# Retention state updates in sets of four, placed between the projection tiles and inside them

## What is computed

```
def retention_chunk(state, q, k, v):
    inner = einsum('bihd,bjhd->bhij', q, k) * dmask
    o = einsum('bhij,bjhv->bihv', inner, v) + einsum('bihd,bhdv->bihv', q, state) * cross_decay
    new_state = chunk_decay * state + einsum('bjhd,bjhv->bhdv', k * k_decay, v)

def retention_output(o, g, gain, w_out):
    on = normalised(o) * gain
    return (silu(g) * on) @ w_out
```

## Time and profile before

| | us |
|---|---|
| median of three timed runs | 1144.43 |
| lowest and highest | 1143.76, 1145.79 |
| the profiled execution | 1144.84 |
| its span, first to last instruction | 1143.1 |
| PE busy in the span | 1088.0 (95%) |
| DVE, ACT busy | 570.1 (50%), 329.8 (29%) |

### The profile page before, as it was taken

One profiled execution on the slowest core, in us unless ns is written; L12 is line 12 of the kernel. 1 busy time (PEld: TensorE's weight loads), 2 busy tenths in 40 slices (PEclk: granted clock), 3 DMA queues, 4 the chain that ended last, 5 costly groups with the idle time before them and its releaser, 6 DMA issues.

```text
span 1143.1 us, 14367 instructions
## 1 busy us (share of the span) xinstructions
PE 1088.0 (95%) x5508; PEld 640.2 (56%) x5508; DVE 570.1 (50%) x1083; ACT 329.8 (29%) x535; POOL 42.5 (4%) x77
## 2 busy tenths in 40 slices
PE   7999999999999999988999999999999999999991
PEld 6877656646443434335888855456787443434330
DVE  6777585656132323229685337648738223323225
ACT  5335256404111111122444313326414111111110
POOL 1300000000000000000000001111000000000000
PEclk9999999998999999999999999999997999999996
DMA  9525281948499999991433478997558599999961
GB/s 325 167 83 182 95 329 61 380 180 317 197 429 406 429 428 428 429 403 63 147 127 107 141 266 304 361 333 274 185 204 338 212 429 406 431 428 428 429 260 47
DMA packets 62890, 319.72 MB, mean 280 GB/s; under 512 B 5026, under 2 KB 5058, under 8 KB 50418
## 3 DMA queue, kind: packets, MB, share of 16 engines
q1 hardware_dynamic: 54386, 288.93, 63.7%
q0 software_dynamic: 8160, 28.80, 6.8%
q10 hardware_dynamic: 288, 1.23, 0.3%
HBM read 296.05 MB, written 22.89 MB: 279 GB/s over the span
## 4 chain that ended last, share of the span: by engine, by line
PE 87%; DVE 6%; DMA 4%; ACT 1%; issue 1%; POOL 0%; SPq 0%; DVEq 0%; ACTq 0%; POOLq 0%
PE bank L1174 31%; PE bank L1006 18%; PE bank L1035 9%; PE bank L966 4%; DMA ring<-in_w_exp_up 3%; PE bank L1494 3%; PE bank L978 2%; PE bank L1241 2%; PE bank L979 2%; PE bank L1484 1%; PE bank L1511 1%; PE bank L944 1%; PE bank L1310 1%; PE bank L1409 1%; PE bank L1395 1%
## 5 line engine op out<-in xcount | busy, mean ns | idle before, releaser
L1174 PE MATMUL bank<-ring_parts,XTt_parts 128*128 128x512 f32 x576 | 181.9, 397 | 2.2 <-DVE ring_parts L2223 1.0
L1174 PE MATMUL bank<-ring_parts 128*128 128x512 f32 x576 | 181.7, 393 | 0.0
L1006 PE MATMUL bank<-ring,XTt 128*64 128x512 f32 x768 | 168.6, 593 | 1.4 <-DMA ring<-in_w_exp_up 1.4
L1174 PEld LDWEIGHTS bank<-ring_parts,XTt_parts 128*128 128x128 f32 x576 | 106.7, 189 | 31.9 <-issue 9.8
L1174 PEld LDWEIGHTS bank<-ring_parts 128*128 128x128 f32 x576 | 107.9, 189 | 24.4 <-issue 1.8
L1006 PEld LDWEIGHTS bank<-ring,XTt 128*64 128x64 f32 x768 | 55.4, 137 | 108.1 <-issue 106.3
L1035 PE MATMUL bank<-ring,arena 128*64 128x512 f32 x512 | 113.4, 595 | 1.7 <-DMA ring<-in_w_exp_down 1.7
L2041 DVE TENSOR_TENSOR arena<-XTt,bank 128x512 f32<-128x512 f32 x16 | 17.3, 1080 | 193.5 <-PE bank L1006 193.5
L707 DVE TENSOR_TENSOR ring_parts<-ring,ring_parts 128x4096 fp32r<-128x4096 f32 x21 | 92.7, 4419 | 23.1 <-ACT ring_parts L696 23.1
L696 ACT ACTIVATE ring_parts<-ring 128x4096 fp32r<-128x4096 f32 (+1 forms) x29 | 84.5, 2916 | 13.8 <-DMA ring<-in_w_in_ret 6.5
L1663 ACT ACTIVATE arena<-bank 128x512 f32<-128x512 f32 (+6 forms) x116 | 53.5, 489 | 88.9 <-PE bank L1174 49.6
(11 more groups left out here) (261 smaller groups left out, 1287.6 us busy)
## 6 DMA issues: line engine op xcount, KB each, us to landing
ring<-in_w_exp_down SPq DMA_DIRECT2D x32, 2048.0 KB, 14.2
ring<-in_w_exp_up SPq DMA_DIRECT2D x32, 2048.0 KB, 14.9
ring<-in_w_exp_gate SPq DMA_DIRECT2D x16, 2048.0 KB, 14.4
arena<-in_w_exp_gate SPq DMA_DIRECT2D x16, 2048.0 KB, 20.0
ring<-in_w_in_ret SPq DMA_DIRECT2D x12, 2048.0 KB, 10.0
ring<-in_state_ret SPq DMA_DIRECT2D x16, 1024.0 KB, 6.6
out_state_s<-ring POOLq DMA_DIRECT2D x16, 1024.0 KB, 5.9
ring<-in_w_in_attn SPq DMA_DIRECT2D x5, 2048.0 KB, 8.3
```

The lines of the kernel that those rows point to most:

```text
L1006: last = pe.matmul(ps[64 * j:64 * j + 64, :], xs[:, k, x0:x0 + 64], w[:, k, :], start=(k == 0), stop=(k == KC - 1))
L1174: last = pe.matmul(ps[:, 0:width], x(t, a, k), w[c][:, k, 0:width], **at)
```

## The change

The states are no longer worked off eight updates at a time. A list `RETENTION` gives one order for PE, DVE and POOL, in which a state's updates are two sets of four (`("update", s, half)`). The sample products (`("so", s)`) stand by themselves in it. A tile with two more numbers, such as `("tile", 0, 1, 0, 1)`, takes a set (here state 0, half 1) in its middle, after 12 of its 24 products, through the argument `lines` of `project`. `banks_of_set` gives the banks: 3, 4, 5, 2, and for the sets (3, 1), (4, 0) and (7, 0) it gives 5, 0, 1, 2. POOL's stores follow set by set. `keys_of(s + 1)` comes after a state's second set. The first tile of n = 3 now stands in the list, with the last set in it. No product, reading or transfer is added or taken away, and SP's order is as it was.

```
-STATES = [(0, 1), (2, 3, 4), (5, 6, 7)]
+RETENTION = ([("head", 0)]
+             + [("tile", 0, 0), ("so", 0), ("update", 0, 0), ("tile", 0, 1, 0, 1), ("so", 1), ("update", 1, 0), ("tile", 0, 2),
+                ("update", 1, 1), ("head", 1)]
+             + [("tile", 1, 0), ("so", 2), ("update", 2, 0), ("tile", 1, 1, 2, 1), ("tile", 1, 2), ("so", 3), ("update", 3, 0),
+                ("head", 2), ("update", 3, 1), ("so", 4), ("update", 4, 0)]
+             + [("tile", 2, 0, 4, 1), ("so", 5), ("update", 5, 0), ("tile", 2, 1, 5, 1), ("so", 6), ("update", 6, 0), ("tile", 2, 2),
+                ("update", 6, 1), ("head", 3), ("so", 7), ("update", 7, 0), ("tile", 3, 0, 7, 1)])
+def banks_of_set(s, half):
+    return (5, 0, 1, 2) if (s, half) in ((3, 1), (4, 0), (7, 0)) else (3, 4, 5, 2)
...
-            def store_state(s):
-                for half in range(2):
-                    wait_emptied(pool, "update", s, 4 * half + 3)
-                    pool.dma_start(state_rows(O["state_s"], s, half),
-                                   weights(("state", s))[:, 4 * half:4 * half + 4, :]).then_inc(state_stored[s][half], 16)
+            def store_state(s, half):
+                wait_emptied(pool, "update", s, 4 * half + 3)
+                pool.dma_start(state_rows(O["state_s"], s, half),
+                               weights(("state", s))[:, 4 * half:4 * half + 4, :]).then_inc(state_stored[s][half], 16)
...
+            def updates(s, half):
                 if s == 0:
                     pe.wait_ge(twice_ready, 3)
                 pe.wait_ge(kd_ready, s + 2)
-                for j in range(8):
+                for j in range(4 * half, 4 * half + 4):
...
-            def gate(n, t):
+            def gate(n, t, *between):
                 if t == 0:
                     pe.wait_ge(low_ready, NIN - 1 + 8 + n)
-                project(fill(("rin", 8 + n, t)), t, x_parts, parts(("rin", 8 + n))).then_inc(full(("rin", 8 + n, t)), 1)
+                project(fill(("rin", 8 + n, t)), t, x_parts, parts(("rin", 8 + n)),
+                        lines=lambda i: updates(*between) if between and i == 2 else None).then_inc(full(("rin", 8 + n, t)), 1)
...
-            head(0)
-            for n in range(3):
-                gate(n, 0)
-                state(STATES[n][0])
-                gate(n, 1)
-                gate(n, 2)
-                state(STATES[n][1])
-                head(n + 1)
-                for s in STATES[n][2:]:
-                    state(s)
+            for what, *of in RETENTION:
+                if what == "head":
+                    head(*of)
+                elif what == "so":
+                    sample_products(*of)
+                elif what == "update":
+                    updates(*of)
+                else:
+                    gate(*of)
...
+                elif what == "tile":
+                    n, t = of[:2]
+                    if of[2:]:
+                        updated(*of[2:])
+                    if n < 3 and t < 2:
+                        gate(n, t)
+                    elif n < 3:
+                        half(n)
```

## The result

| | before | after |
|---|---|---|
| median of the timed runs, us | 1144.91 (6 runs, 1143.76 to 1147.86) | 1154.00 (6 runs, 1151.16 to 1155.60) |
| ratio to before, 95% interval | | 1.0074 (1.0063 to 1.0086) |
| the profiled execution and its span | 1144.84, 1143.1 | 1154.39, 1152.7 |

The change costs 9.1 us by the medians.

The account below looks back on a forecast made before the run. PE, busy 214.05 of 215.00 us, was taken to bound the stage. Sets save 7.9, cuts cost 1.0 and waits 7.9, giving +1.0; the output projection adds 1.6: +2.6, a median of 1147.0, range 1143.5 to 1150.5.

Parts of the forecast that it names:

- A set of four at 1.91: Retention stage: four updates take PE 1.91 us if nothing holds them; over 16 sets this saves 7.9 us.
- The fourth rival: Every set: DVE's pace binds even with empty banks, 2.36 us a set, 1152.4 us; chance 0.05.
- (a): Tiles (0, 2) and (2, 2), right after sets (1, 0) and (6, 0), wait for bank 2: 3.8 us.
- (b): Sets (1, 1) and (6, 1), right after tiles (0, 2) and (2, 2), wait for bank 2: 1.0 us.
- (c): Tile (1, 0) waits for the rest of its weights, done 10.1 after tile (0, 2): 0.4 us.
- (d): Set (4, 0) waits for its keys, which stand late in DVE's list: 0.7 us.
- (e): Tiles (2, 0) and (3, 0) wait for bank 0, second bank of the sets before them: 1.5 us in all.
- (f): State 5 waits for its slot's store and reload after state 3's late half: 0 to 4.6, taken as 0.5 us.
- The other states have over 5 us to spare: Loads of states other than 5 and 6: over 5 us to spare, with POOL and SP transfers in unchanged sequence.
- The output projection's lag: Output projection: DVE and ACT come 3.6 us later against PE, leaving 1.6 us at the last restart; bounds 0 to 3.6.
- The third: Slower than forecast: states 5 and 6 land by the trace's longer times, +2 to +4, 1149.0 to 1151.0 us; chance 0.13.
- The faster rival: Bank waits (a), (b) and (e), 6.3 us, stay away as DVE's readings stay hidden: 1140.7 us; chance 0.12.

Follow-up runs that it names:

- the edit of set (7, 1) alone: Changed kernel with set (7, 1) ahead of tile (3, 0) and not in its middle: 1150.85 us, ratio 1.0052.
- the last run: Changed kernel with states 2 and 4 in one run, set (3, 1) before head 2, (7, 1) before its tile, other banks: 1140.93 us, ratio 0.9969.
- banks_apart: Changed kernel with other banks for the sets of states 1 and 6, apart from bank 2: 1149.54 us, ratio 1.0051.
- reload_after_both_stores: Changed kernel with neither half of states 2 to 7 loaded before both halves of its slot's forerunner are stored: 1155.25 us, ratio 1.0093.

## Why the prediction was wrong in size and right in sign

**A set of four at 1.91:** right, 1.92 in the chain. The fourth rival, DVE's pace for each set, did not come.

**(a), (b), bank 2:** right. Tiles (0, 2) and (2, 2) stand 1.71 us for line 2504 each (forecast 1.7), set (6, 1) took 2.53 (forecast 2.4), and taking both away gave 4.8 us, as summed.

**(c), the rest of tile (1, 0)'s weights:** forecast ready 10.1 after tile (0, 2) and ready at 10.10 (701.50 less 691.40); PE stood 0.1 for it and not 0.4, since set (1, 1) held it a little longer.

**(d), (e):** right. The timeline of PE in after has the keys ahead of set (4, 0), by 0.57, and bank 0 ahead of tile (2, 0), by 0.60 (in brackets, the idle time before):

```profile
739.15 1.99 PE L1506 MATMUL bank<-arena 64*128 64x512 f32 x8 [0.57 <-DVE arena L2497]
...
741.75 0.70 PE L1184 MATMUL bank<-ring_parts,XTt_parts 128*128 128x512 f32 x2 [0.60 <-DVE ring L2504]
```

**(f), the reload of state 5: here it failed.** The forecast took 0.5 from bounds of 0 to 4.6. Its road was right to a tenth: store at 15.41 + 0.26 after tile (1, 2) (measured 738.26 - 722.53 = 15.73), PE there to want it at 27.1 (749.57 - 722.53 = 27.0). And its upper bound, state 5 there at 31.7, is where it landed: 754.27 - 722.53 = 31.74. That close a match is luck: the store took 9.13, more than the 7.8 that the bound had for it, and the load 6.86, less than its 8.2. The wrong step was the choice inside the bounds, 0.5 where its own medians give 28.2 - 27.1 = 1.1, "nearer the small end, because a half is now stored alone and not on the heels of the other". The half was not stored alone. State 2's halves left 4.87 apart, and the second met the first one's reload. State 3's left 10.0 apart, and the second met the first one's reload too, since the first store, held up in turn, took 10.09. The wait was 4.74 in place of 0.5. The medians of 5.9 and 6.6 belong to stores 2.4 apart, and the changed spacing took them out of force: over the sixteen stores of after the landing times, smallest, median and largest, are

```profile
DMA to landing us min/median/max: 4.6/8.1/10.2
```

**"The other states have over 5 us to spare" and the same sequence on SP:** none of them was waited for, but in after state 4 landed only 2.5 us before its products (734.17 against 736.66), and state 7 4.4 before (783.41 against 787.77). SP's sequence was the same, but SP waits in it, and unit 11, behind such a wait, left 5.8 us after its slot was free and ran into the stores of state 3. The forecast named POOL's and SP's order and didn't walk SP's list with the new landing times.

**The clock was not priced.** A forecast that has a wait of up to 4.6 us as a bound has to price what PE does afterwards. The sum had nothing for it. It was 2.4 us, shown by the run that kept PE busy, and half as much again on top of the wait.

**The output projection's lag:** right, 1.4 for 1.6, and the edit of set (7, 1) alone gave exactly that back.

**The rivals.** The third, states 5 and 6 by the longer times, is what happened to state 5: 1147.0 + 4.2 of wait + 2.4 of clock = 1153.6 against 1154.0. It got a chance of 0.13, and its price lacked the clock. State 6 was not late, because PE itself came later by what state 5 had cost; it was late as soon as state 5 was mended. The faster rival needed DVE's readings hidden, 6.3 us; the last run shows that they can be hidden by other banks and another order, and that the loads have to be in time as well before it shows in the time.

## What to carry to other kernels

When a change spreads out the pieces of one buffer's work, redo the transfers' starts, not only their order: write down for each store and load when it leaves and what leaves within a microsecond of it, and walk the issuing engine's list to the first issue that stands behind a late one. A median landing time from the trace holds for the spacing at which it was measured. And a bound that includes a PE wait of several microseconds has to include slower products behind it; here they cost 2.4 us on top of 4.7.

## What the runs showed of the hardware

**A store that starts just behind a load waits for it.** A 1 MB store took 4.6 us alone, 5.9 to 6.0 when it left 2.4 us behind the first half's store and 2.3 to 2.5 ahead of the reload, and 8.2 to 10.4 when it left up to 0.3 us behind a reload that no weight unit ran ahead of (in after and in ten of the other kernels), while the load beside it took 5.9 to 6.6, no more than before. Between 718 and 724 us the load's queue had 528 packets and the store's 88. (The Trainium skill, DMA: Bandwidth & Descriptors, Issuing engines are not separate DMA queues, says that transfers started by different engines run on the same DMA engines and interleave. That they share is what the trace shows; that the sharing is this uneven, it shows too.) Which of the two starts first matters. In the kernel with state 2 in one run, state 5's second store left 0.12 us ahead of a reload, and both were slow (what, queue, KB, us to landing):

```profile
out_state_s<-ring POOLq DMA_DIRECT2D x1, 1024.0 KB, 9.2
ring<-in_state_ret SPq DMA_DIRECT2D x1, 1024.0 KB, 7.8
```

In the last kernel the same store left 0.74 us ahead and took 6.0, and the load took 7.9. Why the sharing is uneven isn't shown. A collision costs time only where something waits for it: in the last kernel state 0's second store still takes 8.7, and nothing waits.

**The clock falls in one wait for a load.** It stood at 1.00 until 748 us; after 4.74 us of waiting the 16 products took 3.64 in place of 1.92, and with the eight updates behind them 2.4 us more than usual. The loss doesn't follow the length of the wait. After waits of 2.47, 3.29, 3.34 and 3.42 products and updates together lost 1.5 to 1.7 us, after 5.53 1.4 (banks_apart), and after 6.43 1.8 (reload_after_both_stores). The 16 products behind the bank waits of 1.71 took 3.94, against 3.87 where the banks were apart, so there the clock was not lower.
